# Expert stage of a two-layer MoE kernel: first products as one 512-column matmul, a 96-place output kept in two banks, scatters by row halves

## The reference

```python
def moe_swiglu(x, router_w, router_b, w1, w3, w2):
    logits = (x @ router_w + router_b).astype(jnp.float32)
    top_v, top_i = lax.top_k(logits, TOP_K)            # 2 of 8 experts a token
    top_p = jax.nn.softmax(top_v, axis=-1)
    gate = jnp.sum(jax.nn.one_hot(top_i, N_EXPERTS) * top_p[..., None], axis=-2)
    out = jnp.zeros_like(x)
    for e in range(N_EXPERTS):
        out = out + gate[..., e:e + 1] * swiglu(x, w1[e], w3[e], w2[e])
    return out

def swiglu(x, w1, w3, w2):                             # 1024 -> 2816 -> 1024
    return (jax.nn.silu(x @ w1) * (x @ w3)) @ w2
```

## Time and profile before

| | us |
|---|---|
| median of 3 runs (2322.94 to 2324.44) | 2323.59 |
| profiled execution, its own time | 2319.97 |
| its span | 2318.7 |
| PE busy | 2205.3 (95%) |
| DVE busy | 695.9 (30%) |
| ACT busy | 427.9 (18%) |

### The profile page before, as it was taken

One profiled execution on the slowest core, in us unless ns is written; L12 is line 12 of the kernel. 1 busy time (PEld: TensorE's weight loads), 2 busy tenths in 40 slices (PEclk: granted clock), 3 DMA queues, 4 the chain that ended last, 5 costly groups with the idle time before them and its releaser, 6 DMA issues.

```text
span 2318.7 us, 36881 instructions
## 1 busy us (share of the span) xinstructions
PE 2205.3 (95%) x16193; PEld 1445.0 (62%) x16193; DVE 695.9 (30%) x1453; ACT 427.9 (18%) x972; POOL 0.2 (0%) x4
## 2 busy tenths in 40 slices
PE   8988999999878999999999999989999999989998
PEld 5664777666755766555455464555667776657775
DVE  2563366223663100110100100035526642730001
ACT  2463000113462000000000100132310002230001
POOL 0000000000000000000000000000000000000000
PEclk9988999999979999999999999989999999999999
DMA  5222987023303999899999887533179641238300
GB/s 217 103 83 102 414 326 286 0 99 134 130 1 143 424 402 388 344 395 407 371 403 419 367 342 312 203 103 116 66 303 397 253 172 55 100 128 334 139 34 19
DMA packets 55175, 523.90 MB, mean 226 GB/s; under 512 B 6368, under 2 KB 6880, under 8 KB 16864
## 3 DMA queue, kind: packets, MB, share of 16 engines
q1 hardware_dynamic: 45792, 471.13, 50.5%
q10 hardware_dynamic: 9216, 50.34, 5.8%
HBM read 520.39 MB, written 1.05 MB: 225 GB/s over the span
## 4 chain that ended last, share of the span: by engine, by line
PE 87%; DVE 7%; ACT 4%; issue 1%; DMA 1%; DVEq 0%; SPq 0%; ACTq 0%
PE ps L89 87%; DVE ring L89 5%; ACT ring L89 2%; DVE stat L89 1%; DVE natural L89 1%; ACT transposed L89 1%; DVE residual L89 0%; ACT L89 0%; DMA ring<-in_moe 0%; DVE transposed L89 0%; ACT z L89 0%; ACT natural L89 0%; ACT stat L89 0%; DMA constants<-in_const 0%; DVE gates L89 0%
## 5 line engine op out<-in xcount | busy, mean ns | idle before, releaser
L89 PE MATMUL ps<-ring 128*32 128x256 f32 (+9 forms) x7764 | 546.4, 338 | 13.6 <-ACT ring L89 3.7
L89 PEld LDWEIGHTS ps<-ring 128*32 128x32 f32 (+4 forms) x7764 | 370.3, 123 | 185.0 <-issue 66.8
L89 PE MATMUL ps<-ring,transposed 128*128 128x384 f32 (+4 forms) x1408 | 473.1, 493 | 4.0 <-ACT transposed L89 4.0
L89 PE MATMUL ps<-ring,z 128*32 128x512 f32 (+3 forms) x2048 | 474.5, 584 | 0.3 <-ACT z L89 0.3
L89 PE MATMUL ps<-transposed,ring 128*128 128x256 f32 x2112 | 466.4, 379 | 5.4 <-ACT transposed L89 4.3
L89 PEld LDWEIGHTS ps<-transposed,ring 128*128 128x128 f32 x2112 | 401.0, 190 | 85.9 <-issue 28.7
L89 PEld LDWEIGHTS ps<-ring,transposed 128*128 128x128 f32 x1408 | 262.7, 192 | 190.7 <-issue 63.7
L89 DVE TENSOR_TENSOR z<-z,ps 128x256 f32<-128x256 f32 (+3 forms) x146 | 58.8, 403 | 889.0 <-ACT z L89 859.2
L89 PEld LDWEIGHTS ps<-ring,z 128*32 128x32 f32 (+2 forms) x2048 | 175.2, 140 | 220.2 <-issue 209.7
L89 ACT ACTIVATE z<-ps 128x256 f32<-128x256 f32 (+2 forms) x151 | 56.4, 373 | 942.9 <-PE ps L89 923.0
L89 ACT COPY z<-ps 128x384 f32<-128x384 f32 (+6 forms) x166 | 68.0, 410 | 653.4 <-PE ps L89 651.8
(11 more groups left out here) (123 smaller groups left out, 923.2 us busy)
## 6 DMA issues: line engine op xcount, KB each, us to landing
ring<-in_moe SPq DMA_DIRECT2D x88, 2048.0 KB, 12.0
ring<-in_ffn SPq DMA_DIRECT2D x66, 1536.0 KB, 13.8
ring<-in_moe SPq DMA_DIRECT2D x88, 1024.0 KB, 10.8
ring<-in_w_in SPq DMA_DIRECT2D x26, 1536.0 KB, 6.3
z<-in_ada ACTq DMA_DIRECT2D x48, 768.0 KB, 6.1
ring<-in_w_out SPq DMA_DIRECT2D x12, 1536.0 KB, 7.0
natural<-in_ada ACTq DMA_DIRECT2D x16, 768.0 KB, 8.1
ring<-in_ple_gate SPq DMA_DIRECT2D x4, 1536.0 KB, 6.5
```

The source lines that it names most:

```text
L89: self.ins = None if self.book.counting else op(*args, **kw)
```

## The change

1. Up is one pass: a matmul's moving operand takes both weights, 256 columns of `w1` and 256 of `w3` that lie 2048 elements apart (`piece_ups`), 512 columns in all. Turn and task stand after block 3 of the width. In the single-block wave it is 2 runs of 128.
2. A 96-place expert takes 9 waves: eight of four block pairs, and one of two jobs with single blocks. The stage has 65 waves.
3. Its outputs lie in banks 2 and 3: the first 64 places as (place, half of the width), the last 32 as (half, parity of the block), two sums that the scatter adds.
4. A scatter of token block `i` does both halves `q` in one task, each half from 64 rows of the array (0 to 63 and 64 to 127) into its own bank, 7 and 4. Gathers and gates are one task each too. 29 tasks are left. The expert with 128 places keeps 128 rows.

```diff
+    def piece_ups(n, k, block, blocks):
+        at = 2 * P * k + (block % 2) * P
+        return piece(n)[:, 0:4 * D].rearrange("p (h n) -> p h n", h=2)[:, :, at:at + blocks * P]
...
-        jobs = [[(t, 2 * p, 2) for p in range(4 * s, 4 * s + 4) for t in range(3)] for s in range(2)]
-        jobs.append([(t, b, 1) for b in range(16, FB) for t in range(3)])
+        pairs = [(t, 2 * p, 2) for p in range(NPIECE) for t in range(3)][0:-1]
+        jobs = [pairs[w:w + 4] for w in range(0, len(pairs), 4)] + [[(2, FB - 2, 1), (2, FB - 1, 1)]]
...
-            for a, b in ((2, 1),) * 6 if CAP[x] == P else ((3, 2), (3, 2), (5, 2)):
+            for a, b in ((2, 1),) * 6 if CAP[x] == P else ((3, 2),) * 3:
...
-    AUX = aux_order()
+    AUX, AUX_BANKS = aux_order(), (7, 4)
...
-    def pe_mo_scatter(x, n, bank_=7):
-        i, q = divmod(n, 2)
+    def pe_mo_scatter(x, i, banks=AUX_BANKS):
         pe.part("mo")
-        pe.wait_ge(f"mo.y{x}", f"mo.gates.done{x}{i}")
-        if CAP[x] == P:
-            rows = [(q, 0, P)]
-        elif CAP[x] == 96:
-            rows = [(0, 0, P), (1, 0, 64)] if q == 0 else [(1, 64, P), (2, 0, P)]
-        else:
-            rows = [(0, 64 * q, 64 * q + 64)]
-        for m, (b, lo, hi) in enumerate(rows):
-            mm(ps[:, bank_, :], mo_gT[lane(x)][lo:hi, i, 0 if CAP[x] == P else b, :], mo_y[lane(x)][lo:hi, b, :],
-               m == 0, m == len(rows) - 1)
-        pe.then_inc(f"mo.scatter{x}{n}")
+        pe.wait_ge(f"mo.y{x}", f"mo.gates.done{x}0")
+        blocks = gate_blocks(x)
+        for b in range(blocks):
+            for q in range(2):
+                lo, hi, at = (0, P, q) if CAP[x] == P else (64 * q, 64 * q + 64, b)
+                mm(ps[:, banks[q], :], mo_gT[lane(x)][lo:hi, i, b, :], mo_y[lane(x)][lo:hi, at, :], b == 0, b == blocks - 1)
+        pe.then_inc(f"mo.scatter{x}{i}")
...
-        for half in range(2):
-            for k in range(KD):
-                for row, width, token, block, n in jobs:
-                    mm(ps[row:row + width, g % 2, half * 2 * P:half * 2 * P + n * P], expert_tokens(x, k)[:, token:token + width],
-                       piece_up(PIECES.index((x, block // 2)), half, k, block, n), k == 0, k == KD - 1)
-            if half == 0:
+        for k in range(KD):
+            for row, width, token, block, n in jobs:
+                mm(ps[row:row + width, g % 2, :].rearrange("p (h n) -> p h n", h=2)[:, :, 0:n * P], expert_tokens(x, k)[:, token:token + width],
+                   piece_ups(PIECES.index((x, block // 2)), k, block, n), k == 0, k == KD - 1)
+            if k == KD // 2 - 1:
...
         if CAP[x] == 96:
-            for a in range(12):
-                block, row = 2 * p + (a // 3) % 2, 32 * (a % 4)
-                mm(ps[row:row + 32, 2 + a // 4, :], turned_block(x, 32 * (a % 3), block), piece_down(n, block, a // 6),
-                   p == 0, p == NPIECE - 1)
+            for b in range(2):
+                for q in range(2):
+                    for t in range(2):
+                        row = 64 * q + 32 * t
+                        mm(ps[row:row + 32, 2, :], turned_block(x, 32 * t, 2 * p + b), piece_down(n, b, q),
+                           p == b == 0, p == NPIECE - 1 and b == 1)
+            for q in range(2):
+                for b in range(2):
+                    row = 64 * q + 32 * b
+                    mm(ps[row:row + 32, 3, :], turned_block(x, 64, 2 * p + b), piece_down(n, b, q), p == 0, p == NPIECE - 1)
...
-        for b in range({P: 2, 96: 3, 64: 1}[CAP[x]]):
+        for b in range(out_banks(x)):
...
-        for n in range(4):
-            pe_mo_scatter(LAST, n, LAST_BANKS[n])
+        for i in range(NT):
+            pe_mo_scatter(LAST, i, LAST_BANKS[i])
```

More of the change, by code:

```diff
@@ L1509, in wave_jobs @@
             return waves + [[(64 * g, 64, 0, FB - 2 + g, 1) for g in range(2)]]
-        jobs = [[(t, 2 * p, 2) for p in range(4 * s, 4 * s + 4) for t in range(3)] for s in range(2)]
-        jobs.append([(t, b, 1) for b in range(16, FB) for t in range(3)])
-        return [[(32 * g, 32, 32 * t, b, n) for g, (t, b, n) in enumerate(part[w:w + 4])] for part in jobs for w in range(0, len(part), 4)]
+        pairs = [(t, 2 * p, 2) for p in range(NPIECE) for t in range(3)][0:-1]
+        jobs = [pairs[w:w + 4] for w in range(0, len(pairs), 4)] + [[(2, FB - 2, 1), (2, FB - 1, 1)]]
+        return [[(32 * g, 32, 32 * t, b, n) for g, (t, b, n) in enumerate(wave)] for wave in jobs]
     def wave_order():
@@ L1543, in aux_order @@
             start = FIRST_WAVE[before(x)] if before(x) is not None else 0
-            waiting += [(2 * FIRST_WAVE[x] - 1, 2 * start, ("gather", x, half), None) for half in range(2)]
+            waiting.append((2 * FIRST_WAVE[x] - 1, 2 * start, ("gather", x, 0), None))
         for x in range(NE):
             b = before(x)
-            waiting += [(2 * LAST_WAVE[x] + 2, 2 * FIRST_WAVE[x] + 2, ("gates", x, i), None if b is None else ("scatter", b, 3))
-                        for i in range(NT)]
+            waiting.append((2 * LAST_WAVE[x] + 2, 2 * FIRST_WAVE[x] + 2, ("gates", x, 0), None if b is None else ("scatter", b, 1)))
             if x != LANES[0][-1]:
-                waiting += [(2 * LAST_WAVE[x] + 16, 2 * LAST_WAVE[x] + 5, ("scatter", x, n), ("gates", x, 1)) for n in range(4)]
+                waiting += [(2 * LAST_WAVE[x] + 16, 2 * LAST_WAVE[x] + 5, ("scatter", x, i), ("gates", x, 0)) for i in range(NT)]
         for slot_ in range(2 * len(WAVES)):
@@ L1602, in pe_route @@
         pe_ple_product(1)
-        for half in range(2):
-            pe_mo_gather(0, half)
+        pe_mo_gather(0)
     def dve_beats(out, x, n):
@@ L1647, in dve_order @@
         dve(V.tensor_copy, most_i, ro_sm[:, 0:1]).then_inc("route.most")
-        for half in range(2):
-            dve_mo_xg(0, half)
+        dve_mo_xg(0)
         dve.part("route")
@@ L1698, in dve_mo_select, with gather_banks, pe_mo_gather, dve_mo_xg @@
         dve.then_inc(f"mo.pick{x}")
-    def pe_mo_gather(x, half):
+    def gather_banks(x):
+        return (6, 7) if x == 0 else AUX_BANKS
+    def pe_mo_gather(x):
         pe.part("mo")
         pe.wait_ge(f"mo.pick{x}")
-        if x == 0 and half == 0:
+        if x == 0:
             pe.wait_ge("ffn1.natural")
[L1706 to L1713, removed]
+        for half in range(2):
+            for k in range(4):
+                for i in range(NT):
+                    at = (4 * half + k) * P
+                    mm(ps[:, gather_banks(x)[half], k * CAP[x]:(k + 1) * CAP[x]], xn[:, i, at:at + P], mo_pick[:, i, 0:CAP[x]],
+                       i == 0, i == NT - 1)
+            pe.then_inc(f"mo.gather{x}{half}")
+    def dve_mo_xg(x):
         dve.part("mo")
         n = CAP[x]
[L1716 to L1727, removed]
+        for half in range(2):
+            dve.wait_ge(f"mo.gather{x}{half}")
+            dve(V.tensor_tensor, mo_xg[lane(x)][:, turn_in_lane(x) % 2, 4 * half * n:(4 * half + 4) * n].rearrange("p (k t) -> p k t", k=4),
+                ps[:, gather_banks(x)[half], 0:4 * n].rearrange("p (k t) -> p k t", k=4),
+                spread(column(1, "g_ffn")[:, 4 * half:4 * half + 4], 2, n), ALU.mult)
+        dve.then_inc(f"mo.gather.done{x}0")
     def dve_mo_weights(x):
@@ L1734, in dve_mo_weights, with out_banks, gate_blocks, pe_mo_gates @@
         dve.then_inc(f"mo.weights{x}")
-    def pe_mo_gates(x, i):
+    def out_banks(x):
+        return 2 if CAP[x] > 64 else 1
+    def gate_blocks(x):
+        return 2 if CAP[x] == 96 else 1
+    def pe_mo_gates(x):
         pe.part("mo")
         pe.wait_ge(f"mo.weights{x}")
[L1739 to L1743, removed]
+        for i in range(NT):
+            for b in range(gate_blocks(x)):
+                turn(AUX_BANKS[i], b * P, mo_pickg[:, i, b, :])
+        pe.then_inc(f"mo.gates{x}")
@@ L1767, in dve_mo_add @@
-    def dve_mo_add(x, n, bank_=7):
+            act.wait_ge(f"mo.scatter{before(x)}1")
+        for i in range(NT):
+            act(S.copy, mo_gT[lane(x)][:, i, 0:n, :], ps[:, AUX_BANKS[i], 0:n * P].rearrange("p (b t) -> p b t", b=n))
+        act.then_inc(f"mo.gates.done{x}0")
+    def pe_mo_scatter(x, i, banks=AUX_BANKS):
+        pe.part("mo")
+        pe.wait_ge(f"mo.y{x}", f"mo.gates.done{x}0")
[5 more added lines that the diff above has]
+        pe.then_inc(f"mo.scatter{x}{i}")
@@ L1768, in dve_mo_add @@
+    def dve_mo_add(x, i):
         dve.part("mo")
-        dve.wait_ge(f"mo.scatter{x}{n}")
-        dve_add_residual(n // 2, n % 2, ps[:, bank_, :]).then_inc(f"mo.scatter.done{x}{n}")
+        dve.wait_ge(f"mo.scatter{x}{i}")
+        for q in range(2):
+            dve_add_residual(i, q, ps[:, AUX_BANKS[q], :])
+        dve.then_inc(f"mo.scatter.done{x}{i}")
     def pe_mo_aux(slot_):
@@ L1779, in pe_mo_aux @@
             else:
-                pe.wait_ge("mo.gather.done01")
-            {"gather": pe_mo_gather, "gates": pe_mo_gates, "scatter": pe_mo_scatter}[kind](x, n)
+                pe.wait_ge("mo.gather.done00")
```

(37 more changed lines are left out.)

18 lines of the change are left out of this document (10 added, 8 removed).

## The result

The changed kernel takes 2287.19 us (median of 4 runs, 2286.13 to 2293.14) against 2324.02 before on the same chip: a ratio of 0.9847 with a 95% interval of 0.9829 to 0.9864. Two later comparisons on other chips gave 0.9868 (0.9852 to 0.9884) and 0.9867 (0.9846 to 0.9888). The medians of the three comparisons differ by 36.8, 31.4 and 31.9 us, 33 on average; forecast were 36.5 us and a time of 2287 us.

What follows compares the result with a forecast made beforehand. PE's own instructions were taken to bound the expert stage. Savings of 25 + 3 + 4 + 5 = 37 us, less 0.5 for the weights, gave 36.5 off 2323.6, so 2287 us, with an 8-in-10 range of 2279 to 2301.

Steps and rivals of the forecast that it cites:

- What bounds the kernel: Expert stage: it lasts as long as PE's instructions do, with DMA the one other engine near its limit.
- Scatters, 25 us: Scatter matmuls of the experts: 64-row halves run in pairs, 50.7 us become 25.6, a saving of 25 us.
- One pass 3 us: Up: merging sets into 512 columns saves 2 to 3 ns each, 3 us together; two runs and weight loads cost nothing.
- forms and tasks 4 us: Expert stage: fewer changes of matmul form, fewer tasks and fewer gate transposes save 4 us together.
- Single-block waves, 5 us: Short waves of 96-place experts: PE waits because the turn stands close behind ACT and DVE; all 5 us go.
- The end, 0: After the last down: fewer copies save 0.6 us, one more add costs 0.7, net 0.
- added waits, 0: Between tasks: PE's new waits for DVE's adds of two banks cost 0, with 2 us as the other end.
- The weights, 0.5 us: Expert pairs: weight transfers at 424 GB/s keep up with PE within 1 us, aided by the ring; charged 0.5 us.
- The weights hold PE: Rival, expert stage: at 402 GB/s the weights take back 13 us, giving 2300 us; chance 12%, in part.
- The scatters pair: Scatters: the two halves run side by side; the rival that they don't takes back 19 us, 2306 us, chance 5%.
- two runs cost nothing: Up's moving operand: no price for two runs; the slower-read rival, chance 4%, gives 2399 us at 0.12 us a set.
- bound at 398: Rival, middle stretches: average transfer at 398 GB/s is the bound, they save nothing, 2308 us; chance 4%.

Runs made afterwards that it cites:

- e9: Changed kernel with both width halves of a 64- or 96-place scatter reading the same array rows, 0 to 63; stage 753.1 us, 18 longer, 0.9938 of the kernel before.
- e7: Changed kernel with up's 512 columns read as one run instead of two (wrong weight columns); stage 734.4 us against 733.7 to 735.4.
- e3: Kernel before with the 9 waves and the one pass together, old scatters kept; stage 752.6 us against 766.1, 0.9958 of the kernel before.
- e1: Kernel before with the 9 waves alone, two passes and old scatter tasks kept; stage 756.8 us against 766.1, 0.9969 of the kernel before.
- e2: Kernel before with up in one pass alone, old waves and scatters kept; stage 756.0 us against 766.1, 0.9968 of the kernel before.
- e10: Changed kernel with up of 96-place experts' double-block waves in matmuls of 128 columns, four times as many; stage 777.1 us, 42 longer, 1.0061 of the kernel before.
- e8: Changed kernel with the down weights' transfer halved from the sixth piece on (other half stale); stage 727.6 us, 6 to 8 less, 0.9839 of the kernel before.
- e6: Changed kernel with scatter matmuls reordered, both of one row half first; stage 736.0 us, 0.9857 of the kernel before.

## Why the prediction was right, and where not

*What bounds the kernel.* Right: PE's own instructions set the stage, and what they lost came off it.

*Scatters, 25 us.* Right. Their busy time fell from 52.8 us to 22.4 + 3.9 over the whole run, 26.5 us, of which 1.6 are the half clock in the last scatters before. e9 gives the 19 us back that pairs are worth (18, or 18.8 without the weights).

*One pass 3 us, forms and tasks 4 us.* The pace was right (0.43 a set, e7 finds no price of two runs). e3 took 13.5 us where the sum has 10 for the same edits. Of the 3.5 us more, 1.6 are the half clock at the end of the stage, which before and e1 have and the others don't; 0.9 is the single-block waves at 5.9 for 5, and the last 1 us no run parts. Half of the weight loads were not free, as the prediction has it: they are half of the instructions that PE ran short of.

*Single-block waves, 5 us.* The size was right (5.9 by e1, e2 and e3) and the cause wrong. I read the turn behind ACT and DVE into rows whose idle time is marked "issue" and stands ahead of matmuls of up. e2 leaves the turn in place and the waits go; e10 has the turn well behind and they come back tenfold (35.0 us against 3.3). PE ran short of instructions, whose packets came too late. That the forecast held in spite of this is luck: the change happens to halve the records where I meant to move the turn.

*The end, 0; added waits, 0.* The end, from ACT's copies on, took 6.4 us (1479.72 to 1486.13) against 10.4; the difference is the scatters' part of the sum and the 1.6 us of half clock before. No wait of PE for DVE's adds shows.

```profile
1479.72 1.20 ACT L89 COPY z<-ps 128x512 f32<-128x512 f32 x2 [2.90 <-PE ps L89]
...
1480.97 3.70 PE L89 MATMUL ps<-z 64*128 64x512 f32 x16 [1.32 <-ACT z L89]
...
1484.72 1.41 DVE L89 TENSOR_TENSOR residual<-residual,ps 128x512 f32<-128x512 f32 x2 [0.31 <-PE ps L89]
```

*The weights, 0.5 us.* This step was mis-sized. They cost 6 to 8 us (after against e8). PE's sum without them is 766.1 - 727.6 = 38.5 us, or 36.9 without the half clock before, and 37 were forecast; with them it is 31 to 32. The two stretches come out the same way: forecast were 167 and 164 us, and they took 171.0 and 167.8, each with one late wait of 3.8 and 3.9 us in it. I compared averages over a pair of experts, 163 us of transfer and 164 of PE, and trusted the ring with the rest. But a ring of five pieces takes in no more than five. In the first half of the pair it was full and the transfers stood nearly still three times (SP waits for PE); from 1000 us on they ran without a gap and were still 2 us late:

```profile
960.00:966.00 6.00, 6.00 (x52) 1.71 (x54) 1.79 (x3) 0.38 (x1) 0.00 (x0) 1.00 0.19 79
990.00:996.00 6.00, 6.00 (x55) 1.60 (x50) 0.42 (x1) 0.38 (x1) 0.00 (x0) 1.00 0.32 90
1000.00:1064.70 64.70, 62.68 (x432) 18.82 (x430) 2.53 (x6) 5.06 (x14) 0.00 (x0) 1.00 1.01 423
```

The six waves from 996.5 to 1062.7 us use ten pieces in 66 us, 6.6 us a piece, where a piece takes 7.4 to land at 424 GB/s. The last five waves of the pair use six. The deficit falls in one place, the seventh wave of experts 1 and 2:

```profile
1059.51 3.17 PE L89 MATMUL ps<-ring,z 128*64 128x512 f32 x14
1064.74 5.34 PE L89 MATMUL ps<-ring 128*32 128x512 f32 x32 [2.06 <-DMA ring<-in_moe]
1070.01 0.44 PE L89 MATMUL ps<-constants,z 128*128 128x128 f32 x2
```

The idle 2.06 us is half of it: the next 32 records take 5.27 us to the next row where 3.57 is usual, 1.7 more, at a granted clock of 0.68 over that stretch, in part the 1.2 GHz level. The wait in expert 2 is 2.22 us and also followed by half clock; together they make 7.7 us, and over e8 this profile has 7.8.

*The rivals.* "The weights hold PE", at 12%, is what happened, at half its price and not by a lower rate (they moved at 423 GB/s while they were late). The scatters pair (e9), two runs cost nothing (e7), and 413 GB/s over the second stretch leaves no bound at 398. That the forecast of 2287 us met the first median to 0.2 us is partly luck: by the two later ratios it would have been 2293 us, still inside the range.

## What to carry to other kernels

Matmuls on different row halves of the array ran side by side here, in both orders of issue that were tried, and a token block of scatters took less than half its time (1.92 us for 4.22). They wrote different banks; whether they must, no run tried. Short matmuls on several column groups at once cost instructions before they cost columns: where PE's idle time ends by "issue" ahead of matmuls without a wait, look whether it ends just after a packet of the instruction queue, and make each matmul longer instead of moving the work around it. And when a saving brings PE near the pace of its transfers, compare the two wave by wave and not on average, with what the ring can hold: here the same waves in another order took 6 us off the stage.

## What the runs showed of the hardware that I had not expected

A record of one row half starts past a record that waits for the other (e6, read from the order of the program: pairs 13 ns apart although issued half by half). PE cannot be fed eight records each 0.11 us for long: 35.0 us idle in 26 places over 32 waves (e10), each ended 1.20 to 1.60 us after a 16 KB packet of instructions landed. The changed kernel's three traces, e6, e7 and e9 have twelve late waits for weights of 2.06 to 3.22 us; eight were followed by 3.4 us at half clock, which adds 1.7 us, and four were not, the longest among them. The clock stood at 1.00 up to each wait. None of e10's 26 idle pieces, up to 2.2 us long, was followed by half clock.
